# First loads in another order, and the conditioning vector spread over the partitions by TensorE in place of a broadcast transfer

## What is computed

```python
def ada_mods(cvec, w, b):
    m = jax.nn.silu(cvec) @ w + b
    return [t[:, None, :] for t in jnp.split(m, 6, axis=-1)]

def post_norm_layer(x, mods, mixer, channel, ln):
    sh1, sc1, g1, sh2, sc2, g2 = mods
    y, state = mixer(x * (1 + sc1) + sh1)
    x = layer_norm(ALPHA * x + g1 * y, ln[0], ln[1])
    x = layer_norm(ALPHA * x + g2 * channel(x * (1 + sc2) + sh2), ln[2], ln[3])
    return x, state
```

## Time and profile before

| | us |
|---|---|
| median of 3 runs | 1589.87 |
| lowest, highest | 1588.78, 1590.74 |
| the profiled execution | 1585.89 |
| its span | 1584.2 |
| between span and time of that execution | 1.69 |
| PE, DVE, ACT, POOL busy | 1492.7, 1260.2, 800.5, 333.6 |

### The profile page before, as it was taken

One profiled execution on the slowest core, in us unless ns is written; L12 is line 12 of the kernel. 1 busy time (PEld: TensorE's weight loads), 2 busy tenths in 40 slices (PEclk: granted clock), 3 DMA queues, 4 the chain that ended last, 5 costly groups with the idle time before them and its releaser, 6 DMA issues. The chain is left out here.

```text
span 1584.2 us, 23836 instructions
## 1 busy us (share of the span) xinstructions
PE 1492.7 (94%) x8783; PEld 1351.9 (85%) x8783; DVE 1260.2 (80%) x1669; ACT 800.5 (51%) x1069; POOL 333.6 (21%) x408
## 2 busy tenths in 40 slices
PE   4999999799999998999999998999999999999996
PEld 1768876599999997997776895999999999999995
DVE  6868788678887986886787845988888888888885
ACT  1222223543233227445677624677676776767763
POOL 2201003700000103002998053010011100110103
PEclk9999999899999999999999798999999999999998
DMA  9535334356566532233321045899999999999961
GB/s 379 186 115 173 134 122 149 100 216 218 215 243 244 216 120 107 107 107 122 104 81 67 1 143 220 310 363 344 370 358 384 348 361 365 379 351 345 367 253 40
DMA packets 50439, 349.68 MB, mean 221 GB/s; under 512 B 6048, under 2 KB 6448, under 8 KB 22720
## 3 DMA queue, kind: packets, MB, share of 16 engines
q1 hardware_dynamic: 31680, 278.88, 45.7%
q0 software_dynamic: 18256, 68.30, 12.8%
q10 hardware_dynamic: 432, 1.57, 0.2%
HBM read 335.22 MB, written 13.50 MB: 220 GB/s over the span
## 5 line engine op out<-in xcount | busy, mean ns | idle before, releaser
L2026 DVE TENSOR_TENSOR arena_r<-arena,arena_r 128x2816 fp32r<-128x2816 f32 x132 | 405.9, 3090 | 48.9 <-ACT arena_r L1130 47.4
L2905 PE MATMUL ps<-arena_r,uT_r 128*128 128x352 f32 (+1 forms) x1188 | 365.5, 308 | 0.0
L1130 ACT ACTIVATE arena_r<-arena 128x2816 fp32r<-128x2816 f32 x132 | 337.4, 2556 | 50.2 <-PE ps L2905 50.2
L2905 PE MATMUL ps<-arena_r,zT_r 128*128 128x352 f32 x1408 | 345.1, 326 | 1.2 <-DVE arena_r L2026 1.1
L2543 PE MATMUL ps<-sqT_r,arena_r 128*128 128x384 f32 x963 | 258.4, 340 | 7.5 <-DVE uT_r L1677 7.5
L2905 PEld LDWEIGHTS ps<-arena_r,zT_r 128*128 128x128 f32 x1408 | 245.6, 188 | 2.0 <-DVE arena_r L2026 1.6
L2905 PEld LDWEIGHTS ps<-arena_r,uT_r 128*128 128x128 f32 x1188 | 223.3, 188 | 0.0
L2543 PEld LDWEIGHTS ps<-sqT_r,arena_r 128*128 128x128 f32 x963 | 177.5, 190 | 8.6 <-issue 8.6
L2905 PE MATMUL ps<-arena_r,spare_r 128*128 128x256 f32 x968 | 176.5, 284 | 4.3 <-DVE arena_r L2026 4.3
L2543 PE MATMUL ps<-arena_r,arena_r 128*128 128x384 f32 x848 | 160.8, 343 | 5.8 <-DVE arena_r L1882 3.2
L2543 PEld LDWEIGHTS ps<-arena_r,arena_r 128*128 128x128 f32 x848 | 150.7, 192 | 8.4 <-DVE arena_r L1882 3.6
(11 more groups left out here) (469 smaller groups left out, 2464.4 us busy)
## 6 DMA issues: line engine op xcount, KB each, us to landing
arena<-in_w_moe SPq DMA_DIRECT2D x132, 1408.0 KB, 7.4
arena<-in_w_up SPq DMA_DIRECT2D x22, 1024.0 KB, 4.8
zT<-in_w_adav POOLq DMA_DIRECT2D x32, 512.0 KB, 4.6
arena<-in_w_xbc SPq DMA_DIRECT2D x12, 1024.0 KB, 4.8
arena<-in_w_down SPq DMA_DIRECT2D x8, 1408.0 KB, 6.1
spare<-in_w_adav POOLq DMA_DIRECT2D x20, 512.0 KB, 5.1
sqT<-in_w_adav POOLq DMA_DIRECT2D x16, 512.0 KB, 3.8
arena<-in_w_z SPq DMA_DIRECT2D x8, 1024.0 KB, 4.8
```

The source lines that it names most:

```text
L1130: nc.scalar.activation(whi[s % PAIRS], slot(s % MRING), ACT.Copy) \
L2026: V.tensor_tensor(wlo[s % PAIRS], slot(s % MRING), whi[s % PAIRS].bitcast(F32), ALU.subtract) \
L2905: m = M.matmul(out, a, b, start=first and n == 0, stop=last and n == 2)
```

## The change

SP issues `cvec` first, then only the identity out of the constants (128 columns), then two tiles `ada0a`; it waits for the identity's landing, issues the rest of the constants and `pvec`, the other two `ada0a` tiles, `xT` and last the masks. POOL's broadcast transfer of `cond` is gone, and so is ACT's SiLU over it. PE fills `crow0` instead: for each of 16 blocks (2 vectors x 8 blocks) one matmul has a column of `cact`, repeated over 128 columns, as its weights and the identity as what streams, which leaves that block's 128 values on every partition. Four such matmuls fill a bank, and DVE copies each of the four banks into `crow0`. DVE's three conversions stand behind `modulate` now, and `modulate` waits for the masks too, since `x_in` counts `cvec`, `xT` and the masks. (`crow[1]`, for layer 1, is loaded by a transfer as before; its waits have other counts.)

```diff
         @block.sync
         def _(sp):
-            sp.dma_start(cons[:, :], i["consts"]).then_inc(S("consts_in"), 16)
-            sp.dma_start(pvec[:, :], i["pvec"]).then_inc(S("consts_in"), 16)
-            sp.dma_start(masks, i["masks"]).then_inc(S("consts_in"), 16)
-            sp.dma_start(cvec, i["cvec"]).then_inc(S("consts_in"), 16)
+            sp.dma_start(cvec, i["cvec"]).then_inc(S("x_in"), 16)
+            sp.dma_start(cons[:, 0:P], i["consts"][:, 0:P]).then_inc(S("consts_in"), 16)
...
                     load(name, width, t, t)
+                    if (name, t) == ("ada0a", 1):
+                        sp.wait_ge(S("consts_in"), 16)
+                        sp.dma_start(cons[:, P:], i["consts"][:, P:]).then_inc(S("consts_in"), 16)
+                        sp.dma_start(pvec[:, :], i["pvec"]).then_inc(S("consts_in"), 16)
...
                 if name == "ada0a":
+                    sp.wait_ge(S("x_in"), 16)
                     sp.dma_start(xT[:, :, :], i["xT"]).then_inc(S("x_in"), 16)
+                    sp.dma_start(masks, i["masks"]).then_inc(S("x_in"), 16)
...
-            gp.dma_start(crow[0], i["cond"].partition_broadcast(P)).then_inc(S("cond_in"), 16)
...
-            act.wait_ge(S("consts_in"), 64)
+            act.wait_ge(S("x_in"), 16)
             nc.scalar.activation(cact, cvec, ACT.Silu).then_inc(S("cact_ready"), 1)
-            act.wait_ge(S("cond_in"), 16)
-            nc.scalar.activation(crow[0], crow[0], ACT.Silu).then_inc(S("cond_ready"), 1)
...
-            v.wait_ge(S("consts_in"), 64)
+            for n in range(4):
+                v.wait_ge(S("cond_ready"), n + 1)
+                step(V.tensor_copy(crow[0][:, n * 512:(n + 1) * 512], ps[:, n, :]))
+            ada_first()
+            v.wait_ge(S("consts_in"), 48)
+            v.wait_ge(S("tr_mm"), ADA_PE)
+            modulations(0, 0, 2 * KB, 1)
+            v.wait_ge(S("x_in"), 48)
+            modulate(0, 0, 0)
             step(V.tensor_copy(maskb16[:, :, :], masks))
...
-            v.wait_ge(S("cond_ready"), 1)
-            ada_first()
-            v.wait_ge(S("tr_mm"), ADA_PE)
-            modulations(0, 0, 2 * KB, 1)
-            v.wait_ge(S("x_in"), 16)
-            modulate(0, 0, 0)
...
             pe.wait_ge(S("cact_ready"), 1)
+            pe.wait_ge(S("consts_in"), 16)
+            for n in range(4):
+                for k in range(4):
+                    m = M.matmul(ps[:, n, k * P:(k + 1) * P],
+                                 cact[:, 4 * (n % 2) + k, n // 2:n // 2 + 1].broadcast_to([P, P]), ident,
+                                 start=True, stop=True)
+                m.then_inc(S("cond_ready"), 1)
```

More of the change, by code:

```diff
@@ L895, in _ @@
                 high(b)
-            act.wait_ge(S("cond_in"), 32)
+            act.wait_ge(S("cond_in"), 16)
             nc.scalar.activation(crow[1], crow[1], ACT.Silu).then_inc(S("cond_ready"), 1)
@@ L1694, in hidden @@
                     .then_inc(S("h_lo"), 1)
-            v.wait_ge(S("cond_ready"), 2)
+            v.wait_ge(S("cond_ready"), 5)
             at = step.n
```

## The result

| | before | changed |
|---|---|---|
| median of 20 runs, us | 1589.84 | 1591.49 |
| lowest, highest | 1585.94, 1592.78 | 1588.68, 1595.08 |
| ratio, 95% interval | | 1.0018 [1.0011, 1.0026] |
| the profiled execution | 1585.89 | 1593.23 |

The change made the kernel slower by 1.7 to 4.1 us (the interval times 1589.8). Forecast were 2.8 us less and a range that ends at 1589.2. The two profiled executions are 7.3 us apart, more than the medians, since that of before was one of the fastest of its kind (4.0 under its median) and that of the changed kernel lay 1.7 above its own. So each stretch is read from the traces, and what it is worth over the whole is read from the medians.

What follows compares the result with a forecast made beforehand. The start of `modulate` (36.62) was taken to set the end. DVE 31.4, `xT` and masks 33.6, PE 33.6 to 34.0 gave 33.8, 2.8 us less: median 1587.1, range 1585.2 to 1589.2.

Steps and rivals of the forecast that it cites:

- What bounds the kernel: First 60 us: everything behind `modulate` (start 36.62) is chained to it, so the kernel's end moves as that start moves.
- the three strands named: Meeting at `modulate`: DVE's products (2.3 us ahead), PE on the `ada0a` tiles (last), `xT`'s landing (close behind PE).
- The broadcast is gone: Queue q0: 1.05 MB less, 2.5 us of all DMA engines; `xT` and masks land at 33.6 instead of 36.1.
- The tiles `ada0a`: Loads on q1: tile 3 lands at 23.8, tile 4 at 28.4 (27.4 to 29.3), before 31.4.
- Rival (b): Loads on q1: constants and `pvec` cost full turns, tile 4 at 30.5, `modulate` 35.7, median 1589.0; chance 0.11.
- PE on them: PE on `ada0a`: at the lower clock after an 8 us gap, tile 3 takes 5.0 not 3.6; `modulate` at 34.0.
- Filling `crow0`: PE's matmuls take about 5.2 us; DVE's products run from 10.4 to 30.7, 2.4 us ahead, so no added gain.
- The conversions: DVE behind `modulate`: 0.29 + 0.23 + 0.23 us hidden in a 1.61 us idle time, costing nothing; uncovered 0.8.
- the sign to look for: Changed profile: first product of `ada_rest` 8.6 us behind the start of `modulate` as before, each later stage about 2.8 sooner.
- the three signs named for being wrong: DVE's products starting past 13, `modulate`'s start moving without the end, or the fourth `ada0a` tile landing past 30.
- Rival (c): Feed of `crow0`: identity or `cvec` lands only at 11.2, `modulate` at 39.9, 3.3 us later, median 1593.2; chance 0.05.
- SP's new waits: SP's load issue: the wait for the identity ends near 4 us with two q1 tiles still to move; nothing starves.

Runs made afterwards that it cites:

- e4: Changed kernel with the broadcast transfer and ACT's SiLU back, PE's 16 matmuls and DVE's four copies out; median 1594.18 us, ratio to before 1.0038.
- e3: Changed kernel with the rest of the constants and `pvec` behind the fourth `ada0a` tile instead of the second; median 1588.78 us, ratio to before 0.9998.
- e7: Changed kernel with 28 more matmuls on PE, results unused, between tiles 2 and 3 of `ada0a`; median 1591.77 us, ratio to before 1.0016.
- e1: Changed kernel with DVE's three conversions moved behind the first four blocks of `ada_rest`; median 1588.89 us, ratio to before 1.0001.
- e2: Kernel before, with only the three conversions moved behind `modulate`; median 1593.92 us, ratio to before 1.0034.
- e5: Changed kernel with the scaling of `xT` done by ACT in place of POOL; median 1586.78 us, ratio to before 0.9990.
- e6: Changed kernel, constants and `pvec` behind the fourth `ada0a` tile, conversions behind four `ada_rest` blocks, `modulate` not waiting for masks; median 1586.07 us, ratio 0.9981.
- e11: The changed kernel run again unaltered; median 1592.23 us, ratio to before 1.0018.

## Why the prediction was wrong

*What bounds the kernel*: right for `modulate`, where the three strands named do meet, and incomplete behind it. "The kernel's end should therefore move as that moment moves" left out that DVE's own chain behind `modulate` can hold PE up: `modulate` moved by 0.8 and the turn by 5.7. Over the 14 runs the median follows the profiled turn with 0.8 us for one (a line fitted through all), and strays from it by 1.6 us (root mean square).

*The broadcast is gone*: right. (The 4.8 us by which q0 was to run out sooner are 4.5 by the moments given for it, 25.7 and 21.2; nothing hangs on it.) `xT` landed at 5.96 + 26.3 = 32.3 and the masks at 6.60 + 27.0 = 33.6, the number forecast for both; with the transfer back the masks came 3.0 later (e4). The masks' turn cost 1.3 us behind `xT`, 1.9 in e3, more than the 0.3 to 1 estimated, but it was inside the 33.6.

*The tiles `ada0a`*: the term was mis-sized. The first tile landed at 9.8 and not 6.6, tile 2 at 14.7 and not 11.5, the constants at 4.05 + 14.4 = 18.5 and not 15.5, `pvec` at 21.2 and not 18.7, tile 3 at 26.1 and not 23.8, tile 4 at about 29.7 and not 28.4. So the turns themselves came as counted or a little quicker (from tile 2 on 3.8, 2.8 and 4.9 us, counted 4.0, 3.2 and 5.1), and the error was in the first tile, which the rest inherited. The 6.6 didn't fit the rows: by 6.6 us both queues together had moved 1.7 MB in the kernel before, and the half of that is less than one tile. In the changed kernel the start was slower still, with 1.05 MB in the first 6 us against 1.47. Rival (b), the order eats the gain, had 0.11; its late tile and more is what happened, though by another sum, and e3 shows that it is the order that costs: there tile 3 came at 19.96.

*PE on them*: the mechanism was right and its size was taken too small. The lower clock was given 1.4 us on tile 3 and cost 2.3 (e7), since the granted clock stayed low for most of the tile and not for its first half; over five profiles it cost 1.4 to 2.4. Only 0.4 of it was let through to `modulate`, because tile 4 was to land last; tile 3 came so late that all of it went through. The two terms together put the additions at 36.6 and not 33.3. The Trainium skill's rule on idle gaps ("TensorE: Matmul & The Clock Gate") sided with the later end here, and by that rule the trace agrees: 0.66 and 0.60 granted behind the gap.

*Filling `crow0`*: right. `cvec` at 2.4, the identity at 4.1, PE's 6.72 us within 3.5 to 7.0 though above the middle value of 5.2, the products from 11.7 (10.4, bounds 8.7 to 12.2). They ended at 32.0, under the other strands.

*The conversions*: this step failed ("they cost nothing"), and by it the sign of the result. I wrote that DVE stood for 1.61 us there, so they cost nothing and 0.8 without the cover. The rows I quoted for it held the refutation: the first product behind the idle time took 5.66 us where its likes took 1.23, with a long instruction of POOL beside it (43.54 to 51.53), and I read its start but not its length. The three conversions took 8.1 us there (0.29, 6.14, 1.70) in place of 0.8. Since the first product no longer had to wait, its end moved by 3.0 (0.8 of it from `modulate`), the late `sqT` tile added 3.5, and the 6.5 us reached PE as the 3.0 of waiting and 1.9 of low clock shown above (e1, e2, e5). The first product began 15.25 us behind `modulate`, where 8.6 "as before" was the sign to look for; none of the three signs named for being wrong stood for this place. Rival (c) looked for the slower side in the feed; no rival was about DVE and POOL together.

*SP's new waits*: right, nothing starved.

Either failure alone was enough to lose the 2.8 us. With only the conversions put elsewhere the median is that of the kernel before (e1, ratio 1.0001), and so it is with only the constants and `pvec` put elsewhere (e3, 0.9998). With both, and without the wait for the masks, it is 3 us lower (e6). The two earlier terms put `modulate` 3.6 us behind the forecast 33.8, and the conversions made of that a loss.

What stays open: the medians move by less than the traces of the first 100 us say for the change itself (5.7 to 5.9 us at the turn, 1.7 to 2.0 between medians, 1.7 to 4.1 by the interval), and e4 came out 3.5 above the line through all and e5 2.5 below, the others within 1.8. The profiled execution is one out of a spread of 7 us; between the two profiles of the kernel before, 2.0 of 2.3 us arise behind the turn. ACT's rows put them between 320 us, where the two profiles are level, and 620, where the second is 2.3 later; the reason is open. Nor was the chain from DVE's L1472 by way of ACT to PE cut by an edit of its own; it is read from the traces.

## What to carry to other kernels

When an instruction is moved, look at what else runs beside its new place, and not only whether its engine is idle there: compare the duration of the instructions that stand there now with those of the same form elsewhere. A row that takes 5.7 us among equals of 1.2 is a price that the next one in that place will pay. Then follow the delay on: an engine with room to spare can still hold up the busiest one through a third engine's order of work, as DVE did PE by way of ACT. And a transfer put between tiles cost 2.8 to 3.8 us here beside the other queue's large rows, for 8 to 506 KB; loads that nobody needs soon go behind the ones that an engine waits for.

## What the runs showed of the hardware

- DVE's first instruction with two SBUF inputs that meets POOL's 128x3072 `tensor_scalar` is held up. One of 1024 columns (1.23 us alone) ends 0.64 to 0.65 us ahead of POOL's end, whenever it starts: 5.66 us long before the change, 7.05 in e1, 4.16 in e6. One of 64 columns (0.23 alone) took 6.14 and ended 1.65 ahead. A conversion with one input took 1.70 behind that in place of 0.23, and ended 0.08 after POOL. The next product, which began with 0.6 us of POOL's left, took its usual 1.22 (before, e1). POOL's own duration moved only from 7.99 to 8.05.
- ACT scales the same 128x3072 in 2.77 us (e5) and DVE beside it runs at full pace.
- After PE had stood for 7.5 us, 16 records took 5.9 us and not 3.6; with 6.5 us of other matmuls in the gap and 1.6 us of standing, 3.61.
- Amid its projections PE stood for 3.00 us (changed), 3.01 (e11) and 2.13 (e2), and the 32 records behind that took 12.2 us with a granted clock of 0.56 to 0.60 near their start; after 2.79 (e3), 1.27 (e7) and 1.15 us (e4) they took 10.56 at 1.00. The length of the gap alone didn't decide.
